# A two-layer attention block and a hybrid block: places of turns, exponentials and projection units around the end of layer one

## The reference

```python
m = rms_norm(mem, mem_norm_g[layer])
mkv = jnp.einsum('bmd,dc->bmc', m, w_mem_kv[layer])
mk, mv = jnp.split(mkv, 2, axis=-1)
...
mixed = jnp.concatenate([o_sb, o_mb, o_mem], axis=-1)
x = x + jnp.einsum('btc,cd->btd', mixed, w_out[layer])
```

## Time and profile before

| | |
|---|---|
| median of 3 runs | 849.33 us (846.13 to 850.15) |
| profiled execution | 849.11 us, span 847.3 us |
| mean granted TensorE clock | 0.989 |
| TensorE matmuls busy | 807.4 us, 95% of the span, 4238 instructions |
| VectorE busy | 495.3 us, 58% |
| ScalarE busy | 469.5 us, 55% |
| GpSimd busy | 130.0 us, 15% |
| DMA | 137.78 MB, mean 163 GB/s |

### The profile page before, as it was taken

The page is one execution under the profiler, slowest core; times in us unless marked ns, Lnnn a source line. Parts: engine busy times, 40 slices in busy tenths (PEclk is TensorE's granted clock), DMA queues, the critical chain, the costliest instruction groups (busy, mean ns, idle before and its releaser), DMA issues.

```text
span 847.3 us, 12690 instructions
## 1 busy us (share of the span) xinstructions
PE 807.4 (95%) x4238; PEld 653.9 (77%) x4238; DVE 495.3 (58%) x731; ACT 469.5 (55%) x1004; POOL 130.0 (15%) x204
## 2 busy tenths in 40 slices
PE   7998999899999999889998999999999999999996
PEld 4777777677777786767777888788887888888884
DVE  5355556566465555856665657666686644455454
ACT  5676476455666654636664666564555533444352
POOL 2011021000234110343334252200000000000000
PEclk9999999999999999989999999999999999999999
DMA  8873543358864365552233344456675736566641
GB/s 256 258 184 110 164 151 105 132 162 262 259 202 125 117 226 170 147 137 84 63 91 96 104 122 143 150 152 224 222 243 176 225 121 191 161 192 186 207 137 50
DMA packets 147295, 137.78 MB, mean 163 GB/s; under 512 B 15025, under 2 KB 115649, under 8 KB 147233
## 3 DMA queue, kind: packets, MB, share of 16 engines
q1 hardware_dynamic: 145136, 129.89, 49.8%
q0 software_dynamic: 2096, 7.09, 2.9%
HBM read 135.90 MB, written 1.05 MB: 162 GB/s over the span
## 4 chain that ended last, share of the span: by engine, by line
PE 71%; ACT 7%; DVE 4%; issue 2%; POOL 1%; ACTq 0%; DVEq 0%; POOLq 0%
PE psum L1163 57%; PE psum L1141 6%; PE psum L1262 3%; ACT w_hi L1444 2%; PE psum L1397 2%; ACT probs L1571 2%; PE psum L1365 1%; PE psum L1183 1%; DVE w_lo L1640 1%; ACT p_t L1589 1%; POOL rtmp L1109 1%; DVE stats L1773 1%; PE psum L1323 0%; ACT xn L1477 0%; ACT gtmp L1614 0%
## 5 line engine op out<-in xcount | busy, mean ns | idle before, releaser
L1640 DVE TENSOR_TENSOR w_lo<-raw,w_hi 128x1024 fp32r<-128x1024 f32 (+1 forms) x234 | 270.1, 1174 | 127.9 <-ACT w_hi L1444 76.2
L1163 PE MATMUL psum<-w_hi,h_hi 128*128 128x512 f32 (+1 forms) x656 | 259.7, 396 | 3.5 <-DVE h_lo L1698 3.3
L1444 ACT ACTIVATE w_hi<-raw 128x1024 fp32r<-128x1024 f32 (+1 forms) x234 | 230.8, 1010 | 48.8 <-PE psum L1163 20.5
L1163 PE MATMUL psum<-w_lo,h_hi 128*128 128x512 f32 (+1 forms) x656 | 247.0, 377 | 0.0
L1163 PE MATMUL psum<-w_hi,h_lo 128*128 128x512 f32 (+1 forms) x656 | 246.4, 376 | 0.0
L1163 PEld LDWEIGHTS psum<-w_hi,h_hi 128*128 128x128 f32 x656 | 124.2, 189 | 30.1 <-issue 13.9
L1163 PEld LDWEIGHTS psum<-w_lo,h_hi 128*128 128x128 f32 x656 | 123.8, 189 | 19.2
L1163 PEld LDWEIGHTS psum<-w_hi,h_lo 128*128 128x128 f32 x656 | 124.5, 190 | 15.5
L1571 ACT ACTIVATE probs<-psum,stats 128x272 f32<-128x272 f32 (+2 forms) x104 | 47.3, 464 | 57.6 <-DVE stats L1765 25.6
L1163 PE MATMUL psum<-w_hi,m_hi 128*128 128x512 f32 x152 | 60.2, 396 | 2.4 <-DVE m_lo L1698 1.5
L1163 PE MATMUL psum<-w_lo,m_hi 128*128 128x512 f32 x152 | 59.3, 390 | 0.0
(11 more groups left out here) (171 smaller groups left out, 999.0 us busy)
## 6 DMA issues: line engine op xcount, KB each, us to landing
raw<-in_w_in SPq DMA_DIRECT2D x112, 256.0 KB, 3.7
raw<-in_w_ffn_in SPq DMA_DIRECT2D x88, 256.0 KB, 4.2
raw<-in_w_in SPq DMA_DIRECT2D x24, 512.0 KB, 4.4
raw<-in_w_out SPq DMA_DIRECT2D x24, 512.0 KB, 3.6
raw<-in_w_in SPq DMA_DIRECT2D x64, 192.0 KB, 2.7
raw<-in_w_ffn_out SPq DMA_DIRECT2D x22, 512.0 KB, 4.6
meta_w<-in_w_in SPq DMA_DIRECT2D x10, 1024.0 KB, 7.7
raw<-in_w_mem_kv SPq DMA_DIRECT2D x8, 512.0 KB, 3.7
```

The source lines that it names most:

```text
L1163: last = nc.tensor.matmul(psum[:, bank, 0:n], sx[name][:, c, t * P:(t + 1) * P], wx[:, kk, 0:n], start=u["first"] and kk == 0 and z == 0, ...
L1444: nc.scalar.activation(weights(u)[0][:, :, 0:n], raw[:, u["raw"], :, 0:n], ACT.Copy)\
L1640: nc.vector.tensor_tensor(lo[:, :, 0:n], raw[:, u["raw"], :, 0:n], hi[:, :, 0:n].bitcast(F32), ALU.subtract)\
```

## The change

Six things are done:

1. `SLOTS` gets `soft` for mb, mem and diff, half a unit behind `scores`; on ScalarE the exponentials of every kind but sb move to `soft` (last hunk). What TensorE and VectorE do at `scores` stays.
2. In layer one the turns of the normalised memory during the first mb group are placed 2, 1, 1 behind its second, third and fourth unit, instead of 1, 2, 1.
3. The units of w_out come in the order a[0], a[1], b[0], b[1], a[2], b[2], in both layers.
4. In layer one `flush` takes the first unit of layer two's memory keys: its tile 0 goes before the last `turn_mix`, tile 1 behind it. The keys' group uses banks 4 and 5 instead of the pair whose turn it is; `banks()` is still called once, so that later groups keep theirs.
5. Of the three other key units the first follows b[3] for tile 1, then the norm of tile 1, the second, the turns of tile 0, the third, the turns of tile 1.
6. The argument of `flush` for the fourth meta group is now a dictionary, and the lines that place the meta loads count in another way.

```diff
--- before.py
+++ after.py
@@ -146,14 +146,15 @@
 SLOTS = {
     "sb": dict(turn_qk=(1,), gate=(1.25, 2.25), scores=(3, 3), later=(4, 4.5), out=(7.75, 7.5),
                turn_mix=(9,)),
-    "mb": dict(turn_qk=(2.5,), gate=(2.25, 4.25), scores=(3, 3), turn_p=(4.5, 5), out=(5.5, 7),
+    "mb": dict(turn_qk=(2.5,), gate=(2.25, 4.25), scores=(3, 3), soft=(3.5, 3.5), turn_p=(4.5, 5), out=(5.5, 7),
                turn_mix=(7.5,)),
-    "mem": dict(turn_qk=(1,), gate=(0.25, 2.25), scores=(1.75, 1.75, 4.25, 4.25), turn_p=(4, 5.25, 6.5, 7.5),
+    "mem": dict(turn_qk=(1,), gate=(0.25, 2.25), scores=(1.75, 1.75, 4.25, 4.25), soft=(2.25, 2.25, 4.75, 4.75),
+                turn_p=(4, 5.25, 6.5, 7.5),
                 out=(5.75, 6.75, 7.75, 8.75), turn_mix=(9.75,)),
     "swa": dict(turn_qk=(3.25, 2.75), scores=(4.45, 4.45, 6.45, 6.45), soft=(4.95, 4.95, 6.95, 6.95),
                 scale=(5.95, 7.95), turn_p=(6.5, 6.5, 8.5, 8.5), turn_tm=(6.5, 8.5), out_t=(7.5, 9.5),
                 mix_t=(7.95, 9.95)),
-    "diff": dict(turn_qk=(1.5, 2.5), scores=(4.25, 4.25), blend=(6.25,), turn_p=(7.75,), out=(8.75,),
+    "diff": dict(turn_qk=(1.5, 2.5), scores=(4.25, 4.25), soft=(4.75, 4.75), blend=(6.25,), turn_p=(7.75,), out=(8.75,),
                  turn_mix=(9.75,)),
 }
 
@@ -198,7 +199,7 @@
 
             for slot in arg:
                 free.appendleft(slot)
-        elif what in ("unit", "unit_a"):
+        elif what in ("unit", "unit_a") or (what == "flush" and arg and "chunks" in arg):
             slot = free.popleft()
             arg["slot"], arg["before"] = slot, user.get(slot, -1)
             user[slot] = len(order)
@@ -260,15 +261,17 @@
             if not arg.get("evac_later"):
                 steps.append(("evac", dict(g=arg, t=0)))
         elif what == "flush":
-            for k in sorted(due):
-                for step in due[k]:
-                    between = arg is not None and step[0] == "turn_mix"
-                    if between:
-                        steps.append(("meta", dict(g=arg, chunks=(0, KC // 2))))
-                    steps.append(step)
-                    if between:
-                        steps.append(("meta", dict(g=arg, chunks=(KC // 2, KC))))
-            due = {}
+            rest = [step for k in sorted(due) for step in due.pop(k)]
+            assert [step[0] for step in rest].count("turn_mix") <= 1
+            for step in rest:
+                between = arg is not None and step[0] == "turn_mix"
+                for n in range(2):
+                    if n:
+                        steps.append(step)
+                    if between and arg["g"]["kind"] == "metakv":
+                        steps.append(("meta", dict(g=arg["g"], chunks=(n * KC // 2, (n + 1) * KC // 2))))
+                    elif between:
+                        part(("unit", "unit_end")[n], arg)
         else:
             steps.append((what, arg))
     assert not due and begun == ended == split == len(order)
@@ -504,12 +507,10 @@
         return (norm(source="mem", dest="mem_n"),
                 [turn for t in range(NT) for turn in norm_turns("mem_n", "m", t)])
 
-    def memory_keys(layer, extra):
-
-        g = pl.group("mkv", banks(), units_of(
+    def key_group(layer, where):
+
+        return pl.group("mkv", where, units_of(
             lambda c: [(0, 1, W["w_mem_kv"][layer], c, 0, 0, 2 * MEMW)], "m"), layer=layer)
-        side(g, extra)
-        return ("turn_mk", dict(mkv=g))
 
     def side(gi, extra):
 
@@ -552,8 +553,10 @@
             line.extend(("unit", u) for u in units[2:])
             side(head_group(layer, "sb", 1), {0: [("masks", None)]})
             side(head_group(layer, "sb", 2), {})
-            side(head_group(layer, "mb", 0), {0: mem_norm, 1: turns[:1], 2: turns[1:3], 3: turns[3:]})
-            turn_keys = memory_keys(layer, {})
+            side(head_group(layer, "mb", 0), {0: mem_norm, 1: turns[:2], 2: turns[2:3], 3: turns[3:]})
+            keys = key_group(layer, banks())
+            side(keys, {})
+            turn_keys = ("turn_mk", dict(mkv=keys))
             side(head_group(layer, "mem", 0), {0: [turn_keys]})
             mem_norm, turns = memory_norm()
             side(head_group(layer, "mb", 1), {0: mem_norm})
@@ -579,16 +582,26 @@
             us[2]["chunks"], us[3]["chunks"] = us[3]["chunks"], us[2]["chunks"]
             us[2]["loads"], us[3]["loads"] = us[3]["loads"], us[2]["loads"]
 
-        line.extend(("unit", u) for u in a[:3] + b[:3])
+        line.extend(("unit", u) for u in a[:2] + b[:2] + a[2:3] + b[2:3])
         if layer == DEPTH - 1:
             metas.append(meta_group(3))
-        line.append(("flush", metas[3] if layer == DEPTH - 1 else None))
+            line.append(("flush", dict(g=metas[3])))
+        else:
+            banks()
+            keys = key_group(layer + 1, (4, 5))
+            line.append(("flush", keys["units"][0]))
         line.extend(("unit_a", u) for u in (a[3], b[3]))
         if layer < DEPTH - 1:
             after = norm(source="x", dest="xn")
             line.append(after[0])
             line.extend(("unit_b", u) for u in (a[3], b[3]))
-            turn_keys = memory_keys(layer + 1, {0: [after[1]], 2: norm_turns("xn", "h", 0), 3: norm_turns("xn", "h", 1)})
+            line.append(("unit", keys["units"][1]))
+            line.append(after[1])
+            line.append(("unit", keys["units"][2]))
+            line.extend(norm_turns("xn", "h", 0))
+            line.append(("unit", keys["units"][3]))
+            line.extend(norm_turns("xn", "h", 1))
+            turn_keys = ("turn_mk", dict(mkv=keys))
         else:
             final, after = norm(source="x", dest="x"), norm(source="x", dest="xn")
             line.append(final[0])
@@ -700,10 +713,10 @@
         for g, u in zip(fo, last_outs):
             line.extend([(name, u), half(final, g, t)])
         line.append(final[t])
-    units = [arg for what, arg in line if what in ("unit", "unit_a")]
+    units = [arg for what, arg in line if what in ("unit", "unit_a") or (what == "flush" and arg and "chunks" in arg)]
     for g in metas:
-        at = line.index(("meta", g) if g["n"] != 3 else ("flush", g))
-        after = sum(what in ("unit", "unit_a") for what, _ in line[:at])
+        at = line.index(("meta", g) if g["n"] != 3 else ("flush", dict(g=g)))
+        after = sum(any(arg is u for u in units) for what, arg in line[:at] if what != "unit_b")
         units[after + META_LOAD[g["n"]]]["then_meta"] = g
     pl.steps = lay_out(line)
     number(pl, pl.steps)
@@ -1546,7 +1559,7 @@
                 elif what in ("scores", "soft"):
                     g = s["g"]
                     kind, j = g["kind"], s["j"]
-                    if (kind == "swa") != (what == "soft"):
+                    if (kind != "sb") != (what == "soft"):
                         continue
 
                     wait(act, s["p_free"])
```

## The result

The changed kernel takes 842.31 us (median of 4 runs, 841.2 to 842.99), the kernel before, on the same chip, 848.52 (4 runs, 846.13 to 850.15). The ratio is 0.9928 with a 95% interval of 0.9900 to 0.9956: faster by 6.2 us or 0.7%. The forecast was 838.3 us, 11.0 us faster, in a range of 833.0 to 844.0. Direction and range hold; the size is off by nearly half.

A forecast was written before the change was run, and what follows sets the result against it. TensorE was taken as the bound, busy 95% of the 847.3 us span, with 40 us to win where it waits. Gains of 17.0 less costs of 6.0 gave 838.1 us, 838.3 by the median; range 833.0 to 844.0.

The forecast's parts named there:

- Fifth meta load: Hung one unit later, its issue waits behind a raw load and it lands 5.0 us later: cost 4.2, bounds 0 and 6.9.
- The other meta loads: First load issued about 4.2 us later, cost 0.4, bounds 0 and 2; nothing put on the second, third and fourth.
- Memory turns: Before the outs of layer one's sb heads: 1.7 us of ring-bank wait and 1.7 of clock gained, 3.4 together.
- rival C: Waits move on to diff heads and mb ring, and one half-clock stretch stays: 843.4 us, chance 0.20.
- Key unit in the chain: Key matmuls fill the holes of 0.73 and 1.02 around turn_mix; with clock, a 0.75 wait and small holes, gain 4.4 us.
- Order of the w_out units: The unit on mix chunks 6 and 7 goes from third to fifth place; its 1.50 wait at 151.78 goes: gain 1.5 us.
- Later exponentials: Exponentials half a unit later gain 1.1 and 1.9 (memory heads), 2.1 (p_t wait), 2.6 (diff heads); mb heads cost 1.4 us.
- A: The sum of the forecast's gains and costs holds: 838.3 us, chance 0.55.
- One of the forecast's own signs of being wrong: The prediction is wrong if the granted clock falls in places that were at full speed in the kernel before.
- B: The fifth meta load isn't late; TensorE waits no more than 2 us before it: 834 us, chance 0.17.
- E: The clock falls more rarely; the two stretches behind 363 and 379 go too, 3.4 us less: 835 us, chance 0.05.
- D: Slower: all meta loads are late, with waits and half clock behind the first three, 19 us: 857 us, chance 0.03.

The follow-up runs named there:

- the first experiment: The changed kernel with all five meta loads back on the units on which they hung before: 833.49 us, ratio 0.9823 to the kernel before.

## Why the prediction was right, and what it missed

The mechanisms are as forecast; the measured gain is 4.8 us smaller than the sum, and the terms say where.

- **Fifth meta load**, forecast 4.2 with bounds 0 and 6.9: this is the term that was mis-sized, and it alone explains most of the miss. All five loads hang one unit later, as was read from the code, and the delay of the issue is the forecast 5.0 (327.06 against 332.27 less the lead of 10.2). Wrong were the three figures behind it. The second half took 8.8 us to land and not the 7.3 of the row; with raw loads issued 0.5 to 1.5 us in front and 1 us behind it takes 8.7 to 9.4 (three profiles), with raw loads 2 to 3 us in front and the next some 3.5 us later 7.3 to 7.5 (all eleven others). That these loads share the DMA engines with it is argued from the windows (share 0.96 to 1.04), not isolated; around the load on time the share is as high (1.08 from 334.5 to 341.5 us in before). The matmuls took 3.62 and not 2.45, 1.2 more, since the clock was low for 10 us; against other profiles with the load on time this would be 0.1 to 1.7. And of the 0.8 to be recovered behind it only 0.5 was. The wait grew by 6.65: 5.0 of issue, 1.5 of landing, 0.15 of the second issue and rounding. 6.65 + 1.2 - 0.5 = 7.35, above the upper bound. By time: 6.7 on the changed kernel, just inside. The fit of the Trainium skill ("DMA: Bandwidth & Descriptors", Anatomy of one DMA) that the forecast weighed gives, as an estimate, 6.8 us for these bytes. No run here agrees with it: the second half landed 7.3 to 9.4 us after its issue.
- **The other meta loads**, forecast 0.4 for the first and nothing for the others. The first was issued 4.2 later, as forecast, but its second half took 10.4 us to land in the changed kernel's profile and not 9.0; the first group waits 0.91, 0.84, 0.47 and 0.42 in the four profiles with that load late. The third group, put at nothing, waits 0.18, 0.53, 0.52 and not at all in the same four. All five loads together cost 7.5 us on the kernel before and, by the ratios 0.9928 and 0.9823, 8.9 on the changed one, where 4.6 was forecast: 3 to 4 of the 4.8 us.
- **Memory turns**, forecast 3.4, measured 1.5 (0.2 to 2.9). The wait fell by 1.6 as forecast; the 1.7 for the half clock was read from one profile in which it happened to be. At 3 in 6 it is worth 0.9 on average, so 2.5 would have been the term, inside the interval. The forecast wrote of rival C that the clock's fall isn't tied to the wait's length alone, and still took the whole stretch into the sum.
- **Key unit in the chain**, forecast 4.4, measured 4.2 (2.5 to 6.0). 2.7 of waits and holes, and 1.7 at 4 in 6, 1.1, make 3.8. That is a little low: where the stretch is absent, the next wait, for x, is longer (1.43 and 1.45 us, against 0.61 to 1.14 where it is there), so without the stretch the place still loses some 3.4, and the average is about 4.1.
- **Order of the w_out units**, forecast 1.5, measured 1.6 (0.3 to 3.1).
- **Later exponentials**, forecast 7.7 less 1.4, measured 7.0 (5.1 to 8.8) together and 3.0 (1.9 to 4.2) for the memory heads where 3.0 was forecast. In the diff heads 2.05 of 2.6 came by the profile, GpSimd's stage taking 0.2 in three of them, and 1.1 was lost again in the 2 us behind them, 0.5 of it at the wait for xn; the 2.1 at p_t came in full, and with it a share of a half clock that the forecast had not counted (3 of 8, 0.6). That makes 3.7 for the diff heads, where the times say 4.5 to 5.7; the difference is within their intervals and has no cause on record. The 1.4 for the mb heads is 1.2 by the profile; the time doesn't tell.
- **In sum**, without the late loads the change is worth 15.0 us (13.2 to 16.9), where the terms gave 15.6. That these are so near is in part luck: the memory turns gave 1.9 less than their term, and the exponentials, 7.0 by the time where 6.3 was forecast, made up for part of it.

Of the rivals, A is what happened but for the load. C's time of 843.4 was nearly met for another reason: the waits did not move on, except for the mb ring (1.20, forecast) and 1.1 us behind the diff heads. One of the forecast's own signs of being wrong did come: around the fifth load the granted clock was low for some 10 us and not for 3.4, so also where it had been at full speed. B and E are out: the load is late; the stretches behind 363 and 379 come and go from profile to profile (one of them stands in the changed kernel, two in its repetition). D is right of the fifth load only. The three kernels with the fifth load on its old unit and the rest of the change (one of them without the mb exponentials), 833.4 to 834.5 us, beat both kernels, before by 1.5 to 1.8% and the changed one by about 1%; the shortest edit that gets there is the one line of the first experiment.

## What to carry to other kernels

When a position is counted from a list (a load hung so many entries on), see what the count includes after a refactoring: a filter that was widened moved five DMA issues that no line of the diff names, and cost half or more of what the edits had won (7.5 to 8.9 of 15.0 us). A transfer with no slack that is queued behind one more load should be priced with its landing in the new neighbourhood, and with the clock that the longer wait leaves to the work behind it. And a stretch at half clock seen once is to be counted with the share of profiles that have it, not in full.

## What the runs showed of the hardware

The granted clock fell to its lower level (1.2 of 2.4 GHz) behind the same wait in some profiles and not in others, in kernels whose steps around that place are the same: 3 of 6 behind 2.16 us, 3 of 8 behind 2.36, and 4 of 6 behind two waits of 0.73 and 1.02 that lie 1.4 us apart, but 10 of 11 behind 2.0 to 2.3 in front of the fifth meta group. During and behind 8.5 to 9.3 us of waiting, three of three profiles had three stretches in a row, mostly while TensorE was idle; what fell on its work in the changed kernel was 1.7 us in the sixteen meta matmuls (3.62, against 1.91 where the clock was full) and 0.6 in the turns behind them (1.60 against 1.03). At the first three of these places no profile had a stretch once the wait was removed (0 of 22). The stretches are also the likeliest source of the kernel's own spread of 846.3 to 852.0 us on one chip, which at 1.7 us a stretch is three or four stretches more or fewer. The 50 runs of the kernel before beside the experiments, on three chips, bear this out: the seven with a mean clock of 0.995 took 845.9 us on average, the six at 0.987 and 0.988 took 849.2, and the one at 0.984 took 852.0.

The landing of a load went with what else was issued around it: the second half of the same 2 MB took 7.3 to 7.5 us in eleven profiles and 8.7 to 9.4 in the three in which raw loads stood close in front and behind.
